# Decoder layer on one core: sample's values in two groups, joint narrow query tiles, other first loads, another order of the last round

## The reference

```python
proj = einsum('btd,de->bte', x, w_in)          # w_in: 1024 x 4096
q, k, v, g_att, b, c, h, g_conv = split(proj)  # 512 columns each
# attention: three causal branches (window, dilation) (128,1) (512,4) (2048,16),
# each a softmax; merged with weights proportional to their denominators
o_att = dilated_attention(q, k_all, v_all, offset)
att = o_att * silu(g_att)
u = c * h                                      # short convolution, width 3
z = b * (w0*u[t] + w1*u[t+1] + w2*u[t+2]) * silu(g_conv)
out = einsum('bte,ed->btd', concat([att, z]), w_out)
y = layer_norm(alpha * x + out) * ln_g + ln_b
# also returned: the new k, v caches and conv states
```

## Time and profile before

| | |
|---|---|
| Median of 3 runs | 373.02 us (372.99 to 373.15) |
| Profiled execution, own time | 373.99 us |
| Its span, first to last instruction | 372.2 us |
| PE (TensorE) busy | 356.4 us, 96% |
| PEld (weight loads) | 313.2 us, 84% |
| DVE / ACT / POOL busy | 202.6 / 119.0 / 20.4 us |
| DMA packets | 141.06 MB, mean 379 GB/s |
| Chain that ended last | PE 86%, DMA 6%, DVE 3%, ACT 2% |

### The profile page before, as it was taken

The page is one execution under the profiler, slowest core; times in us unless marked ns, Lnnn a source line. Parts: engine busy times, 40 slices in busy tenths (PEclk is TensorE's granted clock), DMA queues, the critical chain, the costliest instruction groups (busy, mean ns, idle before and its releaser), DMA issues.

```text
span 372.2 us, 7719 instructions
## 1 busy us (share of the span) xinstructions
PE 356.4 (96%) x3266; PEld 313.2 (84%) x3266; DVE 202.6 (54%) x379; ACT 119.0 (32%) x242; POOL 20.4 (5%) x32
## 2 busy tenths in 40 slices
PE   6899999999999999999999999999999979999992
PEld 5799888899998888999988889998778968888781
DVE  3634436864134648641346486413437889394864
ACT  4633413442134324421443244214343653220000
POOL 0000000000100000001000000010000055200000
PEclk9999999999999999999999999999999998999997
DMA  7999999999999995999999999999999999999961
GB/s 214 404 417 422 424 415 417 411 396 415 403 418 417 419 364 201 364 407 404 400 418 408 421 410 386 422 421 395 417 416 417 414 414 316 377 343 375 368 235 56
DMA packets 36196, 141.06 MB, mean 379 GB/s; under 512 B 3521, under 2 KB 5441, under 8 KB 34113
## 3 DMA queue, kind: packets, MB, share of 16 engines
q1 hardware_dynamic: 19698, 73.20, 49.7%
q10 hardware_dynamic: 16464, 67.37, 46.5%
HBM read 135.80 MB, written 71.86 MB: 558 GB/s over the span
## 4 chain that ended last, share of the span: by engine, by line
PE 86%; DMA 6%; DVE 3%; ACT 2%; SPq 1%; issue 0%; ACTq 0%; DVEq 0%
PE pj_b L1099 10%; PE pj_a L1099 10%; PE pj_b L1101 8%; PE pj_b L1100 8%; PE pj_a L1100 8%; PE pj_a L1101 8%; PE sc L1221 5%; PE sc L1257 5%; DMA wo_raw<-in_w_out 4%; PE px L1421 3%; PE px L1423 3%; PE px L1422 3%; PE po L1200 3%; PE px L1170 3%; PE pt L1187 2%; DMA k_buf<-in_xT 2%
## 5 line engine op out<-in xcount | busy, mean ns | idle before, releaser
L1099 PE MATMUL pj_a<-x_hi,w_hi 128*128 128x288 f32 x256 | 79.3, 310 | 3.3 <-DVE x_lo L761 3.3
L1099 PE MATMUL pj_b<-x_hi,w_hi 128*128 128x288 f32 x256 | 79.2, 309 | 2.6 <-DVE mix L869 2.6
L1100 PE MATMUL pj_b<-x_lo,w_hi 128*128 128x288 f32 x256 | 76.2, 298 | 0.0
L1101 PE MATMUL pj_b<-x_hi,w_lo 128*128 128x288 f32 x256 | 76.0, 297 | 0.0
L1100 PE MATMUL pj_a<-x_lo,w_hi 128*128 128x288 f32 x256 | 75.6, 295 | 0.0
L1101 PE MATMUL pj_a<-x_hi,w_lo 128*128 128x288 f32 x256 | 75.3, 294 | 0.0
L1099 PEld LDWEIGHTS pj_a<-x_hi,w_hi 128*128 128x128 f32 x256 | 48.1, 188 | 12.1 <-issue 8.5
L1099 PEld LDWEIGHTS pj_b<-x_hi,w_hi 128*128 128x128 f32 x256 | 48.6, 190 | 6.7 <-DVE mix L869 2.8
L448 ACT CAST w_hi<-w_raw 128x1024 fp32r<-128x1024 f32 x30 | 31.4, 1046 | 56.9 <-PE pj_b L1101 42.0
L754 DVE TENSOR_TENSOR w_lo<-w_raw,w_hi 128x1024 fp32r<-128x1024 f32 x30 | 36.7, 1222 | 22.9 <-ACT w_hi L448 22.9
L1100 PEld LDWEIGHTS pj_b<-x_lo,w_hi 128*128 128x128 f32 x256 | 48.8, 191 | 0.0
(11 more groups left out here) (143 smaller groups left out, 440.5 us busy)
## 6 DMA issues: line engine op xcount, KB each, us to landing
k_buf<-in_k_used SPq DMA_DIRECT2D x16, 1280.0 KB, 12.8
v_buf<-in_v_used SPq DMA_DIRECT2D x40, 512.0 KB, 17.2
out_k_used_out<-in_k_used ACTq DMA_DIRECT2D x16, 1280.0 KB, 13.7
out_v_used_out<-in_v_used ACTq DMA_DIRECT2D x20, 1024.0 KB, 13.9
w_raw<-in_w_tiles SPq DMA_DIRECT2D x30, 512.0 KB, 10.9
out_k_rest_out<-in_k_rest ACTq DMA_DIRECT2D x12, 1024.0 KB, 11.3
out_v_rest_out<-in_v_rest ACTq DMA_DIRECT2D x12, 1024.0 KB, 11.2
wo_raw<-in_w_out SPq DMA_DIRECT2D x8, 512.0 KB, 17.3
```

What stands on the lines that cost most here:

```text
L1099: nc.tensor.matmul(out, w_hi[:, w], x_hi[:, c], start=(k == 0), stop=False)
L1100: nc.tensor.matmul(out, w_hi[:, w], x_lo[:, c], start=False, stop=False)
L1101: return nc.tensor.matmul(out, w_lo[:, w], x_hi[:, c], start=False, stop=(k == KT - 1))
```

## The change

- `sample_values`: tiles 0 to 4 before `project(q_tile)`, 5 to 9 after both halves of it, in rounds 1 to 3.
- Query tiles 2 and 3 of the prompt become one step (`STEPS`): scores, masks, exps, norms, transposes, copy and values are done together, side by side in the same 384 columns.
- First loads: six x chunks, four weight chunks; the first two weight tiles come from an array of their own, `w_first`, in runs of 2048 bytes.
- Last round: `sample_scores` and `prompt_values` change places; `split_wo` and `split_wo_lo` stand at other places; pieces 4 and 5 of w_out get their low part on DVE, behind `split_mix_lo(1)`, and POOL keeps 6 and 7. Two copies move from the last round's start to round 2.
- `x_res` has five places, and all five loads are issued at once.

```diff
-X_CHUNKS = ((0, 0, 1), (0, 1, 2), (0, 2, 4), (0, 4, 6), (0, 6, 8), (1, 0, 2), (1, 2, 4), (1, 4, 8))
-W_CHUNKS = 5
+STEPS = ((0,), (1,), (2, 3))
+N_STEPS = len(STEPS)
+X_CHUNKS = ((0, 0, 2), (0, 2, 4), (0, 4, 6), (0, 6, 8), (1, 0, 4), (1, 4, 8))
+W_CHUNKS = 4
...
+        def unit_cols(u):
+            c0 = width(2) if u == 3 else 0
+            return c0, c0 + width(u)
...
             for n, (h, k0, k1) in enumerate(X_CHUNKS):
                 if n < W_CHUNKS:
-                    sp.dma_start(two_tiles(w_raw, k0, k1), d["w_tiles"][0:2 * P, k0 * P:k1 * P]
-                                 .rearrange("(s p) n -> p s n", s=2)).then_inc(w_first_in[n], 16)
+                    c = slice(2 * k0 * P, 2 * k1 * P)
+                    sp.dma_start(w_raw[:, c], d["w_first"][:, c]).then_inc(w_first_in[n], 16)
...
             for t in range(QT + 1):
                 rows = P if t != SAMPLE_AT else NS
-                if t >= 2:
-                    sp.wait_ge(r_done, 2 * (t - 1))
...
+                sp.dma_start(x_res[0:rows, t * 1024:(t + 1) * 1024], d["x_rows"][y_rows(t), :]).then_inc(res_in[t], 16)
...
-            for n in range(NHP, KT):
+            for n in range(KT - 2, KT):
                 pool.wait_ge(wo_hi_done, n + 1)
...
+            split_x(4)
             split_x(5)
-            split_x(6)
             stage_v(0)
-            split_x(7)
...
             (act_round)
                 split_hi(t0 + 4)
                 copy_next()
+                if i == 1:
+                    copy_next()
                 exp_gate(t0 + G_CONV, 0)
                 move_prompt(i, 2)
                 copy_next()
-                exp_prompt(i, 3)
                 exp_gate(t0 + G_CONV, 1)
...
-                move_prompt(i, 3)
-                copy_next()
+                copy_next()
+                if i == 1:
+                    copy_next()
...
             (act_last_round)
                 split_hi(t0 + 2)
-                copy_next()
                 move_prompt(i, 0)
...
                 split_wo(2)
-                split_wo(3)
                 exp_gate(t0 + G_CONV, 1)
                 split_mix_first()
                 copy_next()
+                split_wo(3)
+                exp_gate(gate_tile(i), 0)
+                copy_next()
                 split_wo(4)
                 split_wo(5)
-                copy_next()
-                exp_gate(gate_tile(i), 0)
+                exp_gate(gate_tile(i), 1)
+                split_mix(1)
                 copy_next()
                 split_wo(6)
                 split_wo(7)
                 copy_next()
-                exp_gate(gate_tile(i), 1)
-                split_mix(1)
                 out_sample(i)
...
             (dve_last_round)
                 split_lo(t0 + 4)
+                z_read(i)
+                gate_half(i, 0, 0)
                 split_wo_lo(0)
                 split_wo_lo(1)
-                z_read(i)
-                gate_half(i, 0, 0)
-                split_wo_lo(2)
-                split_wo_lo(3)
                 gate_half(i, 0, 1)
                 split_mix_first_lo()
+                split_wo_lo(2)
                 gate_half(i, 1, 0)
+                split_wo_lo(3)
+                gate_half(i, 1, 1)
                 split_mix_lo(1, 1)
-                gate_half(i, 1, 1)
+                split_wo_lo(4)
+                split_wo_lo(5)
...
             (pe_round)
                 prompt_turn(i, 2)
-                prompt_scores(i, 3)
...
-                prompt_turn(i, 3)
                 project(v_tile(i + 1), 1)
-                prompt_values(i, 3)
...
-                sample_values(i, 0)
-                sample_values(i, 1)
+                for t in range(0, 5):
+                    sample_values(i, t)
                 project(q_tile(i + 1), 0)
-                sample_values(i, 2)
-                sample_values(i, 3)
                 project(q_tile(i + 1), 1)
...
             (pe_last_round)
                 prompt_scores(i, 1)
+                sample_scores(i, 1)
                 prompt_values(i, 0)
-                sample_scores(i, 1)
                 project(t0 + H, 0)
                 prompt_turn(i, 1)
                 prompt_scores(i, 2)
+                sample_scores(i, 2)
                 prompt_values(i, 1)
-                sample_scores(i, 2)
                 project(t0 + H, 1)
                 prompt_turn(i, 2)
-                prompt_scores(i, 3)
-                prompt_values(i, 2)
                 sample_scores(i, 3)
                 project(t0 + B, 0)
-                prompt_turn(i, 3)
+                prompt_values(i, 2)
                 pe.wait_ge(u_done, i + 1)
                 project(t0 + B, 1)
-                prompt_values(i, 3)
```

More of the change, by code:

```diff
@@ L145, in layer_step @@
         small_in, ln_in, ln_spread = sem("small_in"), sem("ln_in"), sem("ln_spread")
-        res_in = [sem("res_in0"), sem("res_in1")]
+        res_in = [sem(f"res_in{t}") for t in range(QT + 1)]
         wo_in = [sem(f"wo_in{n}") for n in range(KT)]
@@ L229, in width, with step_width @@
             return (QT - u) * P
+        def step_width(s):
+            return sum(width(u) for u in STEPS[s])
+        def unit_cols(u):
+            c0 = width(2) if u == 3 else 0
+            return c0, c0 + width(u)
         def out_banks(t):
@@ L380, in _ @@
                 rows = P if t != SAMPLE_AT else NS
-                if t >= 2:
-                    sp.wait_ge(r_done, 2 * (t - 1))
[L383 to L389, removed]
+                sp.dma_start(x_res[0:rows, t * 1024:(t + 1) * 1024], d["x_rows"][y_rows(t), :]).then_inc(res_in[t], 16)
+            for t in range(QT):
+                sp.wait_ge(ln_done, t + 1)
+                rows = P if t != SAMPLE_AT else NS
+                sp.dma_start(d["y"][y_rows(t), :], y_t[0:rows, t % 2 * 1024:(t % 2 + 1) * 1024])\
+                    .then_inc(y_out[t % 2], 16)
             sp.wait_ge(ln_done, QT + 1)
@@ L1184, in prompt_turn @@
                         pe.wait_ge(s_moved, 4 * i)
-                    for k in range(QT - u):
+                    for k in range(step_width(s) // P):
                         c = e * SEQ + k * P
@@ L1188, in prompt_turn, with prompt_values @@
                     last.then_inc(pr_turned, 1)
-            def prompt_values(i, u):
-                n = QT * i + u
-                t = QT - 1 - u
-                pe.wait_ge(pr_moved, 2 * n + 2)
-                if u == 0 and i:
-                    pe.wait_ge(pr_out, i)
-                for k in range(t + 1):
-                    for e in range(2):
-                        v = k * P + e * 64
-                        last = nc.tensor.matmul(po[e * 64:e * 64 + 64, t * P:(t + 1) * P], v_rows[:, v:v + 64],
-                                                pt_pr[:, e * SEQ + k * P:e * SEQ + (k + 1) * P],
-                                                start=(k == 0), stop=(k == t))
+            def prompt_values(i, s):
+                pe.wait_ge(pr_moved, 2 * (N_STEPS * i + s) + 2)
+                if s == 0 and i:
+                    pe.wait_ge(pr_out, i)
+                for u in STEPS[s]:
+                    t = QT - 1 - u
+                    for k in range(t + 1):
+                        for e in range(2):
+                            v = k * P + e * 64
+                            c = e * SEQ + unit_cols(u)[0] + k * P
+                            last = nc.tensor.matmul(po[e * 64:e * 64 + 64, t * P:(t + 1) * P], v_rows[:, v:v + 64],
+                                                    pt_pr[:, c:c + P], start=(k == 0), stop=(k == t))
                 last.then_inc(pr_pv, 1)
```

138 lines of the change are left out of this document (71 added, 67 removed).

## The result

The changed kernel takes 367.55 us (median of 4 runs, 365.99 to 367.70) against 373.00 for the kernel before: a ratio of 0.9844, 95% interval 0.9817 to 0.9871, so 5.4 us or 1.5% faster. Forecast were 363.9 us, range 360.3 to 368.2. Timed again with the experiments, the same kernel gave 0.9828 (0.9781 to 0.9874). The sign and the range hold; 3.6 us of the 9.1 in the sum are missing.

A forecast was written before the change was run, and what follows sets the result against it. TensorE was taken as the bound, busy 74.48 of 74.48 us in the third round. Savings of 3.0 + 1.8 + (6.2 - 2.9) + 1.0 = 9.1 us off the 373.02 us median gave 363.9, range 360.3 to 368.2.

The forecast's parts named there:

- Sample's values in two groups: Three rounds: five groups of sample values become two, each pair joined saving 0.33 us; 3.0 us saved in all.
- Joint narrow query tiles: Three rounds: merging the prompt's narrow query tiles saves 0.6 us a round, 1.8 in all, bounds 0.9 and 2.4.
- First loads: Kernel start: fewer x chunks and larger weight rows bring between 0.4 us lost and 3.3 won; 1.0 taken.
- Last round, up to the gate: Last round before the output projection: removed waits, merged groups and an avoided clock fall together save 6.2 us.
- (b): Last round: two groups merge as in the earlier rounds; 0.6 us saved.
- (c): Last round: reordered w_out splits remove TensorE's wait before project(gate,1); 2.56 us saved, 1.0 if still late.
- (d): Last round, after the wait at the gate: without that wait the clock doesn't fall to 0.50; 1.5 us saved.
- (a): Last round: ready work placed ahead of prompt_values removes TensorE's two waits for pt_pr; 1.5 us saved.
- rival (3): Transfers don't follow, ACT waits for weight tiles, the last round's 6.2 us come back in part: 368.5 us; chance 0.12.
- Rival (5): Slower: transfer backlog plus two added copies delays round 3's tiles; costs nothing up to about 4 us; 375 us; chance 0.03.
- Output projection: Its second part waits for DVE's low parts, stretched beside POOL; 2.9 us lost, bounds 0 and 5.
- rival (2): Output projection: DVE and POOL meet, TensorE waits 3 us or more, clock falls; 1.5 to 2 more, 365.7; chance 0.17.

The follow-up runs named there:

- tile B's cast moved: Changed kernel with the last round's split of the B weight tile moved behind move_prompt(1) and conv_in(0): 368.68 us, ratio 0.9886.
- both orders: Changed kernel with gate_half(1,1) moved behind DVE's low parts and the last round's B weight tile split later: 364.45 us, ratio 0.9758.
- two copies late: Kernel with both orders, two 1 MB copies taken out of the last round and issued at the first two layer-norm steps: 363.08 us, ratio 0.9780.
- the second execution: Profiled execution of the changed kernel, run again with no edit: 365.32 us; that timing's median was 365.46 us.
- four copies late: Changed kernel with four 1 MB copies moved from the last round to behind the output projection's start: 369.69 us, ratio 0.9926.
- groups undone: Changed kernel with sample values of rounds 0 to 2 again in five groups of two key tiles: 367.71 us, ratio 0.9877.

## Why the prediction was right in sign and range, and 3.6 us too good

**Sample's values in two groups:** 3.0 forecast, 2.92 measured twice, once added and once removed. The price of a visit to a smaller tile, 0.33 us from the earlier trace rows, is right.

**Joint narrow query tiles:** 1.8 forecast, and 5.08 - 2.92 = 2.16 as the remainder, inside the bounds of 0.9 and 2.4. No run has this part alone.

**First loads:** forecast 1.0. The first C starts 1.12 us earlier in the profiled execution (28.39 for 29.51), which agrees by luck. With the loads as before it also started at 28.39 once, and over the twelve profiled executions with the new ones it lies anywhere from 27.84 to 29.03. The start moves by a microsecond from run to run; the loads alone gave a ratio of 0.9996. What they bring is within the noise of these runs.

**Last round, up to the gate:** forecast 6.2, measured from C to the output projection's first product (312.37 - 252.83) - (302.08 - 246.63) = 4.09. (b), (c) and (d) came as worked out: no wait at the gate, no fallen clock there. (a) is the term that was mis-sized: 1.5 saved were forecast, a wait of 2.1 stands there, and 6.2 - 2.1 = 4.1 is the measured gain. Where the wait is taken away (tile B's cast moved, both orders, two copies late) this stretch is 53.3 us, 6.2 shorter than before, just the forecast. The step knew `split_hi(t0 + 2)` ahead of that copy on ScalarE, but not that it would stand there for a transfer. That is rival (3)'s mechanism ("in part", 0.12), at one place. The term that failed under it is the two moved copies, priced at 0 "if that hole is really used". The hole was used (share 0.98), and the copies still delayed tile B, by 6.5 of the 6.9 us by which it comes later against TensorE. Rival (5) had expected 3.5 us of this, and nothing to happen up to 4.

**Output projection:** forecast 2.9 for meeting POOL. From its first to its last product it takes 358.15 - 302.08 = 56.07 us, where the kernel before took 364.70 - 312.37 = 52.33: 3.74 more, and 2.18 more in the second execution, whose clock did not fall. In the 3.74 are 1.57 + 0.12 of waiting and 1.6 of fallen clock; 0.45 has no row. That is rival (2)'s mechanism, with half its wait. That 2.9 lies between 2.18 and 3.74 is partly luck: it was counted as waiting alone. That POOL stretches DVE's operations is shown by the kernel without its subtractions (2.41 becomes 0.68). That the wait is not the transfers is shown by w_out's last tile, which landed at 292.0 us with four copies late and was cast only at 305.63 with the groups undone, with a wait of 1.6 us both times. That the wait goes when POOL makes no low parts is not shown, since the broadcasts took their place; it goes when DVE's order is changed.

**The sum against its own execution.** 373.99 - 9.1 = 364.9 forecast for a profiled execution; measured 367.70. Of the 2.8 us, 2.1 are the new wait at L1220, 0.8 the output projection's 3.74 for 2.9, and 0.25 a tail of 7.35 us behind the last product instead of 7.1; the rounds give back 0.3 and the first loads 0.1. The median is a further 0.8 us off, because that execution of the kernel before lay 0.97 above its median and that of the changed one 0.15 above.

**What was wrong beyond one term.** The sum was made as if its parts were independent. They are not: 2.92 us saved in the rounds, correctly forecast, were worth less than nothing in the kernel before, and taken out of the changed kernel they cost 1.2 to 1.8. That it is the reordered last round (c) that lets a part of them reach the end is likely, since the wait that swallowed them is gone with it, but no run has that reordering alone. And (a) could not bring more, because the kernels that removed its wait got it back at the output projection (3.3 and 5.3 us for 1.6), unless the order there was mended with it.

## What to carry to other kernels

A saving ahead of a wait may be worth nothing; price the wait again with everyone arriving earlier: ask what its last releaser hangs on (here ScalarE's cast, for a transfer in full queues, and DVE beside POOL), and whether that moves with the saving. When a wait falls on an engine, list what stands ahead of the late instruction on it, the transfers too. And a transfer moved into a hole costs nothing only if the hole is still as large with the change's other parts in place (here the share was 0.76 before, and 0.84 with the shorter rounds), and if the queues drain before the next tile that is wanted at a set time; look at that tile's landing.

## What the runs showed of the hardware that I had not expected

- The same wait of 1.57 us of TensorE was followed by a fallen clock (0.50) in one execution of the same kernel and by none in another; nor did it fall after the 2.12 us wait at `prompt_values(0)` (granted clock 1.00 from 261 to 264 us). Among the other kernels it fell behind waits of 1.56 us (four copies late), 0.77 and 1.14 (POOL makes no low parts) and 0.46 and 1.43 (both orders), and not behind one of 1.58 (groups undone). With 3.3 and 5.3 us of waiting it fell in both profiled executions, already before the wait ended.
- A DVE operation of 0.2 us (128x64) took 2.38 us beside a POOL subtraction, and one of 0.69 us took 2.3 to 2.4. The price is not in proportion to the operation: the 128x64 product ended 0.1 us and the 128x512 subtraction 0.6 us after POOL's, so it is what was left of POOL's. The Trainium skill (SBUF - State Buffer, section SBUF: two separate sides) says so: of a DVE instruction with two SBUF inputs and a GpSimd one that reads SBUF, the one which starts first keeps the shared port pair for its whole length. By that rule the traces agree. That POOL's partition broadcasts cost DVE time as well (6.55 us for four subtractions of 1.2) no part of the forecast had.
- With six or seven copies of 1 MB under way from ScalarE's queue, three further issues took 9.4 us, and the next three 9.7, instead of 0.6 us each, and ScalarE's next instruction waited behind them. In the changed kernel two issues took 8.2 us as well (from 306.30), where nothing of ScalarE was wanted yet.
